# A two-layer mixer trunk whose x, memory and result are laid out feature by feature outside the program

## The reference

```
h      = rms_norm(x) * ln_g
u      = h @ w_in                       # q, k, v, z of four branches, f, and 4 x 1024 gates
mkv    = (rms_norm(mem) * mem_ln_g) @ w_mem_kv
o_b    = attention_b(...)               # stick-breaking, forgetting, dilated, memory
y_b    = (o_b * silu(z_b)) @ w_b
merged = sum over b of sigmoid(gate_b) * y_b
x      = x + merged @ w_out
```

## Time and profile before

| | us |
|---|---|
| median of 3 runs | 1245.41 |
| lowest, highest | 1244.69, 1245.96 |
| the profiled execution | 1244.55 |
| its span, first to last instruction | 1242.8 |
| PE busy in it | 1223.4 (98%) |
| DVE, ACT, POOL busy | 633.5, 681.3, 684.8 |

### The profile page before, as it was taken

One profiled execution on the slowest core, in us unless ns is written; L12 is line 12 of the kernel. 1 busy time (PEld: TensorE's weight loads), 2 busy tenths in 40 slices (PEclk: granted clock), 3 DMA queues, 4 the chain that ended last, 5 costly groups with the idle time before them and its releaser, 6 DMA issues.

```text
span 1242.8 us, 18333 instructions
## 1 busy us (share of the span) xinstructions
PE 1223.4 (98%) x6378; PEld 992.0 (80%) x6378; DVE 633.5 (51%) x1125; ACT 681.3 (55%) x1301; POOL 684.8 (55%) x563
## 2 busy tenths in 40 slices
PE   7999999999999999999999999999999999999998
PEld 6888888777777888887888888887777788888876
DVE  6788533876745222223349874357676442222221
ACT  6775544776554544544458744357755454544531
POOL 3675523574343676776457664237634346776762
PEclk9999999999999999999999999999999999999999
DMA  7654422222222344443365443122222224444342
GB/s 225 171 134 127 102 52 59 60 69 69 65 56 68 98 115 103 106 114 111 102 168 148 126 119 85 44 55 74 60 69 60 60 73 118 102 115 102 103 119 85
DMA packets 209891, 120.83 MB, mean 97 GB/s; under 512 B 9736, under 2 KB 200328, under 8 KB 209800
## 3 DMA queue, kind: packets, MB, share of 16 engines
q1 hardware_dynamic: 209800, 119.66, 37.0%
HBM read 107.04 MB, written 6.29 MB: 91 GB/s over the span
## 4 chain that ended last, share of the span: by engine, by line
PE 92%; DVE 3%; ACT 2%; POOL 1%; issue 1%; DMA 0%; SPq 0%; DVEq 0%; ACTq 0%; POOLq 0%
PE dense L842 76%; PE score L842 6%; PE out L842 4%; PE acc L842 3%; PE acc L1149 1%; PE turn L842 1%; POOL w_lo L1816 1%; POOL dk_lo L1879 1%; PE turn L1000 0%; DMA sig<-in_x 0%; ACT w_hi L1266 0%; PE acc L1000 0%; PE score L953 0%; ACT h_hi L1233 0%; DVE o_norm L1580 0%
## 5 line engine op out<-in xcount | busy, mean ns | idle before, releaser
L1816 POOL TENSOR_TENSOR w_lo<-w_raw,w_hi 128x512 fp32r<-128x512 f32 (+1 forms) x400 | 498.2, 1252 | 519.2 <-ACT w_hi L1266 461.1
L842 PE MATMUL dense<-h_hi,w_hi 128*128 128x512 f32 (+1 forms) x1176 | 473.1, 402 | 2.6 <-DVE h_lo L1457 1.8
L842 PE MATMUL dense<-h_lo,w_hi 128*128 128x512 f32 (+1 forms) x1176 | 457.1, 389 | 0.0
L842 PE MATMUL dense<-h_hi,w_lo 128*128 128x512 f32 (+1 forms) x1160 | 450.9, 389 | 0.0
L842 PEld LDWEIGHTS dense<-h_hi,w_hi 128*128 128x128 f32 x1176 | 221.0, 188 | 59.1 <-issue 11.2
L1266 ACT ACTIVATE w_hi<-w_raw 128x512 fp32r<-128x512 f32 (+1 forms) x401 | 231.6, 585 | 66.2 <-PE dense L842 65.9
L842 PEld LDWEIGHTS dense<-h_hi,w_lo 128*128 128x128 f32 x1160 | 217.7, 188 | 46.7
L842 PEld LDWEIGHTS dense<-h_lo,w_hi 128*128 128x128 f32 x1176 | 221.3, 188 | 39.6 <-issue 0.2
L1552 DVE TENSOR_TENSOR sig<-dense,x_rstd_row 128x512 f32<-128x512 f32 x48 | 33.2, 692 | 215.0 <-issue 122.7
L1326 ACT ACTIVATE sig<-sig 128x512 f32<-128x512 f32 x48 | 30.4, 633 | 127.9 <-DVE sig L1552 127.9
L1554 DVE TENSOR_TENSOR raw<-dense,x_rstd_row 128x512 f32<-128x512 f32 x80 | 54.8, 685 | 29.3 <-issue 18.4
(11 more groups left out here) (297 smaller groups left out, 2030.2 us busy)
## 6 DMA issues: line engine op xcount, KB each, us to landing
w_raw<-in_w_in SPq DMA_DIRECT2D x292, 256.0 KB, 2.9
w_raw<-in_w_out SPq DMA_DIRECT2D x32, 256.0 KB, 2.8
x_scratch<-v_dil SPq DMA_DIRECT2D x16, 256.0 KB, 3.5
w_raw<-in_w_mem_kv SPq DMA_DIRECT2D x16, 256.0 KB, 3.0
v_dil<-x_scratch SPq DMA_DIRECT2D x16, 256.0 KB, 2.8
turned<-normed SPq DMA_DIRECT2D x48, 64.0 KB, 2.5
inv_den<-o_norm SPq DMA_DIRECT2D x48, 64.0 KB, 2.6
silu_z<-in_mem SPq DMA_DIRECT2D x4, 512.0 KB
```

What stands on the lines that cost most here:

```text
L842: return nc.tensor.matmul(o, lhsT, rhs, start=start, stop=stop, skip_group_check=True)
L1816: pool.tensor_tensor(w_lo[:, g % SPLIT_SLOTS, c], w_raw[:, g % RAW_SLOTS, c], f(w_hi[:, g % SPLIT_SLOTS, c]), ALU.subtract).then_inc(w_lo_ ...
```

## The change

1. The host lays out `x`, `mem` and the result with features down; the program loads `x` straight into `xT`, one `kt` at a time, with the first weight item ahead and the second among them. All transposes of `x`, of memory and of the result go. The stores of the result leave from `xT`.
2. Layer 0 makes `h` and the first tile on all 512 tokens. The squares are now made by ACT on `xT` (8 of them) and summed by DVE (7 additions), alternating with `h_hi` and `h_lo`. `x_sum` of layer 0 is the product that layer 1 has, at the table's place, which is inside the first tile.
3. Memory isn't scaled. ACT squares it in four pieces, POOL adds them up (3 additions a layer), PE sums them with two products of 256 columns (`mem_sum`), ACT makes the row of roots, and DVE multiplies it in when it takes `mk` and `mv` from PSUM. `mem_hi` and `mem_lo` are made from SBUF.
4. Layer 0 saves no `x`; it loads it back from the input.
5. The table gets two rooms behind the first `col` and two ahead of the first `rv`; the addition of memory's last gated output goes from POOL to DVE; the last tile of the result is added and stored in two halves.
6. The values' buffers lose their ones (two memsets of POOL).

```
@@ plan_layer
                 yield unit
                 unit = []
+                if s == 0 and e == 0:
+                    yield from [room()] * 2
...
             if s < len(order):
                 yield both("rd", s)
+            if s == 1:
+                yield from [room()] * 2
...
-          [room(), [("x_sum",)]] + [room()] * 6 + [[("mem_square",)]] + [room()] * 2 + [[("mem_scale",)]] + [room()], lag=2)
+          [room(), [("x_sum",)]] + [room()] * 4 + [[("mem_square",)]] + [room()] * 2 + [[("mem_rest",)]] + [room()] * 2 + [[("mem_sum",)]] + [room()], lag=2)
...
-                          ([("mem_t", c)] + ([("mem_low", c - 1)] if c else []), room())] + [[("mem_low", 3)], room()], lag=2)
+                          ([("mem_high", c)] + ([("mem_low", c - 1)] if c else []), room())] + [[("mem_low", 3)], room()], lag=2)
...
-    dense([new("o", None, dt) for dt in range(HALF + 1)])
-    add("out", 0)
-    dense([new("o", None, dt) for dt in range(HALF + 1, KT - 1)])
-    dense([new("o", None, KT - 1)], [room(), [("out", 1)]])
-    add("out", 2)
+    dense([new("o", None, dt) for dt in range(KT)])
@@ sync
-                    if n in saves:
+                    if n in saves and l:
...
+            for kt in range(KT - 1):
+                sp.wait_ge(*x_new.of(kt))
+                sp.dma_start(out[:, kt, :], xT[:, kt, :]).then_inc(out_stored, 16)
+            for i in range(2):
+                c = slice(i * MEM, (i + 1) * MEM)
+                sp.wait_ge(x_last, i + 1)
+                sp.dma_start(out[:, KT - 1, c], xT[:, KT - 1, c]).then_inc(out_stored, 16)
@@ tensor
                         if l:
-                            wait(pe, turn_ring.before("x_sum"))
                             pe.wait_ge(*x_summed.of(KT - 1, ago=1))
-                            mm(T[:, :], ones, turned[:, :], start=True, stop=True).then_inc(x_total.sem, 1)
                         else:
...
+                            pe.wait_ge(first_summed, KT - 1)
+                        mm(T[:, :], ones, turned[:, :], start=True, stop=True).then_inc(x_total.sem, 1)
+                    elif kind == "mem_sum":
+                        wait(pe, turn_ring.before("mem_sum"))
+                        pe.wait_ge(*mem_added.of(3))
+                        for i in range(2):
+                            last = mm(T[:, 0:MEM], ones, sig[:, 0, i * MEM:(i + 1) * MEM], start=i == 0, stop=i == 1)
+                        last.then_inc(mem_total.sem, 1)
@@ scalar
             first_split(0)
             act.wait_ge(params_in, 16 * DEPTH)
             first_high(0)
+            first_high(1)
+            first_square(0)
+            first_high(2)
             first_split(1)
+            for kt in range(3, KT):
+                first_square(kt - 2)
+                first_high(kt)
             first_split(2)
+            first_square(KT - 2)
+            first_square(KT - 1)
@@ vector
             for kt in range(KT):
+                first_low(kt)
+                if kt >= 3:
+                    first_add(kt - 2)
+            first_add(KT - 2)
+            first_add(KT - 1)
...
+                            if t.branch == MM and t.idx == KT - 1:
+                                a = acc[t.idx % 2][:, :]
+                                dve.wait_ge(*y_gated.of(t.n))
+                                dve.wait_ge(*y_added.before(t.n))
+                                dve.tensor_tensor(a, a, gated[gated_ring.slot(t.n)], ALU.add).then_inc(y_added.sem, 1)
@@ gpsimd
+                    elif kind in ("mem_square", "mem_rest"):
+                        for c in (1, 2) if kind == "mem_square" else (3,):
+                            pool.wait_ge(*mem_squared.of(c))
+                            if c >= 2:
+                                pool.wait_ge(*mem_added.of(c - 1))
+                            pool.tensor_tensor(sig[:, 0, :], sig[:, 0, :], mem_square_place(c), ALU.add).then_inc(mem_added.sem, 1)
```

More of the change, by code:

```diff
@@ L781, in _ @@
             stage = flat(probs[:, :, :])
+            sp.dma_start(stage[:, 0:P], c_square[:, IDENT, :]).then_inc(const_in, 16)
             sp.dma_start(stage[:, P:9 * P].rearrange("p (a b) -> p a b", b=P), c_square[:, HEADSUM:, :])\
@@ L903, in qk_there @@
                     once(qk_lo_ready.of(tile_at[kind, branch, idx]))
-                def first_tile():
-                    for u in range(2):
-                        c = slice(u * MEM, (u + 1) * MEM)
-                        for kt in range(KT):
-                            half, i = divmod(kt, HALF)
-                            if u == 0 and i == 0:
-                                pe.wait_ge(w_lo_ready, half + 1)
-                            pe.wait_ge(first_h_lo[u], kt + 1)
-                            part = slice(i * P, (i + 1) * P)
-                            last = three(dense_bank[0][:, c], w_hi[:, half, part], w_lo[:, half, part],
-                                         h_hi[:, kt, c], h_lo[:, kt, c], u == 0 and kt == 0, u == 1 and kt == KT - 1)
-                            if u == 1 and i == HALF - 1:
-                                last.then_inc(w_used, 1)
                 for s in steps:
@@ L921, in _ @@
                     if kind == "x_sum":
+                        once((setup, 2))
+                        wait(pe, turn_ring.before("x_sum"))
                         if l:
-                            wait(pe, turn_ring.before("x_sum"))
                             pe.wait_ge(*x_summed.of(KT - 1, ago=1))
-                            mm(T[:, :], ones, turned[:, :], start=True, stop=True).then_inc(x_total.sem, 1)
                         else:
-                            pe.wait_ge(first_squares, TT)
@@ new lines, in _ @@
+                    elif kind in ("mem_square", "mem_rest"):
+                        act.wait_ge(mem_in, 64 * (l + 1))
+                        for c in range(3) if kind == "mem_square" else (3,):
+                            if c == 3:
+                                act.wait_ge(*mem_added.of(1))
+                            act.activation(mem_square_place(c), memT[:, c, :], ACT.Square).then_inc(mem_squared.sem, 1)
+                    elif kind == "mem_sum":
+                        act.wait_ge(*mem_total.of(0))
+                        act.activation(mem_rstd_row[:, :], T[:, 0:MEM], ACT.Ln, scale=1.0 / D, bias=eps).then_inc(mem_rstd.sem, 1)
+                        act.wait_ge(*mem_rstd.of("ln"))
+                        act.activation(mem_rstd_row[:, :], mem_rstd_row[:, :], ACT.Exp, scale=-0.5).then_inc(mem_rstd.sem, 1)
@@ L1510, in _ @@
                     kind = s[0]
-                    if kind == "out":
-                        if l < DEPTH - 1 or s[1] == 1:
-                            continue
-                        a = s[1] // 2
-                        for i in (0, 2):
-                            dve.wait_ge(out_turned, a * TT + i + 1)
-                            dve.tensor_copy(token_stage(i)[:, a * S:(a + 1) * S], (R[0], O)[i // 2][:, :])\
-                                .then_inc(out_copied[0], 1)
-                    elif kind == "mem_low":
+                    if kind == "mem_low":
                         c = s[1]
@@ L1583, in _ @@
                                 dve.wait_ge(x_back, 16 * KT * (l + 1))
+                            if (l, t.idx) == (DEPTH - 1, KT - 1):
+                                for i in range(2):
+                                    c = slice(i * MEM, (i + 1) * MEM)
+                                    dve.tensor_tensor(xT[:, t.idx, c], bank_[:, c], xT[:, t.idx, c], ALU.add).then_inc(x_last, 1)
+                                continue
                             dve.tensor_tensor(xT[:, t.idx, :], bank_[:, :], xT[:, t.idx, :], ALU.add)\
@@ L1855, in _ @@
                         pool.tensor_tensor(cosine_place(t), normed_place(t), rope[:, 0, :], ALU.mult).then_inc(cos_done.sem, 1)
-                    elif kind == "post1" and s[1].kind == "y" and s[1].branch != DIL and not last_y(s[1]):
+                    elif kind == "post1" and s[1].kind == "y" and s[1].branch != DIL and not last_y(s[1]) \
+                            and (s[1].branch, s[1].idx) != (MM, KT - 1):
                         t = s[1]
@@ L1905 @@
           for k, v in arrays.items()}
-    result = nc.dram_tensor("result", (S, D), F32, kind="ExternalOutput").ap()
+    result = nc.dram_tensor("result", (P, KT, S), F32, kind="ExternalOutput").ap()
     def rows_split(w):
@@ L1917 @@
     r = run_bass_kernel_spmd(nc, [arrays], core_ids=[0])
-    return r.results[0]["result"].reshape(1, S, D)
+    return r.results[0]["result"].reshape(P, KT, S).transpose(2, 1, 0).reshape(1, S, D)
```

236 lines of the change are left out of this document (67 added, 169 removed).

## The result

| | before | after |
|---|---|---|
| median of the runs, us | 1245.1 (4 runs beside those of after) | 1257.1 (4 runs) |
| lowest, highest | 1244.7, 1246.0 | 1256.8, 1257.9 |
| ratio, 95% interval | | 1.0097 (1.0085 to 1.0109) |
| the profiled execution, its span | 1244.55, 1242.8 | 1257.44, 1255.6 |

A forecast was written before the change was run, and what follows sets the result against it. PE, busy 98% of the span, was taken as the bound. Terms -1.4 (memory), -3.1, -2.2, -2.2, -0.6 make -9.5, with the head +1.6 -7.9: 1236.7, stated as 1237.0 us for the median; range 1232.5 to 1241.

The forecast's parts named there:

- Turning the result: Result transposes out 0 and out 1, between dense matmuls on PE: their removal saves 1.76 and 1.33 us, -3.1.
- memory's transposes: Four groups of four transposes on PE in each of two layers, 0.455 us each: their removal gives -3.6 us.
- The sum: All terms added: -9.5, or -7.9 with the head at +1.6; 1236.7 plus 0.9 for the median, stated as 1237.0 us.
- The end: From DVE's last addition to the span's end: half additions and split stores save 2.2 us, between 1.6 and 2.8.
- The last sum: PE's wait for the last sum, 0.6 us a layer, shrinks with memory's last addition on DVE: -0.6, half of -1.2.
- The head: Start of layer 0: PE waits at x_sum until 17.9 us, then runs at half speed, losing 2.5 us; net +1.6.
- two products for +2.2: mem_sum on PE, two plain float32 products of 256 columns a layer: 1.1 us a layer, +2.2, at most 3.5.
- The 20 gaps that become a triple shorter: Table places shortened by the rooms, 0.68 us each: PE shows no wait of size there, so nothing taken.
- The rival that had it in view: Shortened table gaps: 40 lose 0.68 us, 27 us if none had slack, 1264; decides from 16 on; chance 0.05.
- The table: Rooms at the second col and first rv remove PE waits of 0.7 and 0.4 us in each layer: -2.2.
- DVE behind POOL's additions: Rival, 50 to 75 us: three additions a layer cost DVE 0.65 us each, 1240; chance 0.20 shared with no table help.
- The signs named as wrong: PE waiting for raw<-dense between 50 and 110 us, new waits at sb_sum or rv, or squares done before 14 us.

The follow-up runs named there:

- e3: The changed kernel with layer 0's x_sum run on PE after 36 matmuls, in the middle of the second tile, not after 15: 1251.5 us.
- e4: The changed kernel with mem_sum in a score bank, the last two sb_sum together and layer 0's x_sum after 36 matmuls: 1239.45 us.
- e1: The changed kernel with mem_sum's two products put into a score bank of PSUM, not the turn bank: 1254.8 us.
- e2: The changed kernel with the two sb_sum steps of the last stick-breaking block standing together in the table: 1248.2 us.
- e7: The kernel before with only the two rooms behind the first col added: 1252.6 us, ratio 1.0056.
- e8: The kernel before with only the two rooms ahead of the first rv added: 1244.6 us against 1244.8.
- e10: e9 with the three additions of memory's squares in each layer on DVE, not POOL: 1235.3 us.
- e12: e4 with squares' additions on DVE, mem_high and mem_low at places 20 to 45, squares at 93 to 111, mem_low reading ACT's PSUM copy: 1234.6 us.
- e9: e4 with ACT copying memory into a score bank of PSUM, from which DVE's mem_low reads: 1237.8 us.
- e5: e4 with the mem_high and mem_low steps moved into the first group of tiles, the squares ahead of them: 1239.4 us.

## Why the prediction was wrong

- **Turning the result, -3.1; memory's transposes, -3.6.** The rows are gone, and nothing took their place on PE. Right by the trace; no run had them alone.
- **The sum.** 1236.7 and 0.9 are 1237.6, not 1237.0: a slip of 0.6, small beside the 20 us.
- **The end, -2.2.** It gave 3.6: 3.1 us from DVE's last additions, not 4.5. The stores were issued 1.3 us after the additions began (1.45 forecast), the queue waited 1.4 us for the last landing and not 2.3, and the span ends 0.5 behind that, not 0.7.
- **The last sum, -0.6.** PE's wait for the low part of the last sum, 0.6 us in each layer, is no longer in its list, so it is nearer to -1.2. Its row stands beside other edits, so this is not separated.
- **The head, +1.6.** It cost 2.75 us (24.70 against 21.95). The mechanism was that of the forecast, waiting and then half speed, but the wait was 6.05 us and not 4.5. Mis-sized is the chain of DVE: its last addition ended at 19.8 and not at 17.9. DVE waited 2.6 us for `h_hi` of the next three `kt`, not 0.7 (the second `kt` was there at 6.85), and its last three additions took 3.35, not 2.1, since the last square had to wait for a place that an addition frees. Half speed lost 1.7 us (nine matmuls from 20.98 to 24.70 for 2.05), not 2.5. `e3` shows that PE needn't wait there at all: in `e4` PE's first head sum starts at 27.2 us, in the kernel before at 30.2, in after at 32.9.
- **Memory: two products for +2.2, at most 3.5 "if both halves wait for POOL's last addition".** The first of two steps that failed. The products themselves were not the error: in `e4`, layer 0, they cost 0.87 us (53.15 to 54.47, less two pitches) for 1.1. I asked whether its *input* would be late and never asked who holds its *output* bank. 3.8 us a layer of waiting, and half speed behind it, came from a bank whose reader ACT is a tile behind. `e1` shows the bank as the cause of the wait; what the wait cost in time, it shows at 1.8 us only. The kernel before had put the transposes into the score banks.
- **The 20 gaps that become a triple shorter: "so I take nothing".** The second step that failed, and the costliest: 8.5 us by `e2`, and 7.8 without the rest of the change by `e7`. The rival that had it in view got 0.05 and was priced as 40 gaps of 0.68 us, to decide from 16 of them on. It was not a shorter gap that cost, but one pair of steps with two foreign steps slipped in between, and one such place in each layer is enough: its price is the length of the chain that slipped in (3 us, and half speed behind it), not the shift (0.68). "Only the two mended places show a wait" was no argument, since the other places had slack only in the order that they had.
- **The table, -2.2.** The wait at `col` and that at `rv` went as forecast. What the first brought is not shown, since `e7` has the new wait with it; of the 0.8 us for `rv`, `e8` shows 0.2, with an interval that holds both nothing and 0.8.
- **DVE behind POOL's additions, 0.65 each, 1.5 a layer.** Seen as a rival and in the right stretch, but too small and on the wrong operation: I noted that `mem_low` now reads SBUF and put no price on it. Eleven of its sixteen products took 1.0 us more, 5.7 us a layer. In after little of it showed in PE's waits, with the pauses there; in `e4`, without them, PE has some 7 us of new waits (w_lo 3.9 for 1.9, raw 2.8, square 2.2), and `e10` is 5.6, `e12` 6.3 us better than `e4`.
- **The clock.** A wait on PE has a second price that I had applied at the head alone. After a pause of 3 to 4 us PE ran at half speed for up to 6.2 us more (911.80 to 918.02, behind `sb_pv` of layer 1), and seven matmuls at 0.43 us lose 1.4.

The signs named as wrong came true in part: a new wait in the stick-breaking part, though at `sb_pv`, and in `e1` and `e4` PE's waits for `raw<-dense`.

## What to carry to other kernels

When a step is put into a fixed order, ask of both of its ends: who still holds the buffer that it writes, and not only whether its inputs are there. When units in such an order move by one place, list which pairs of steps that belong together now have a foreign step between them, and price each with the foreign step's whole chain. And when an operand moves from PSUM to SBUF, take the new operation's duration from a row with the same places for its operands and with POOL busy beside it, above all if it stands ahead of the step that frees a bank for PE.

## What the runs showed of the hardware

- A DVE product of 256 columns with both tensors in SBUF took 476 ns where POOL stood idle as it started and about 1.5 us (median 1504) where POOL was at work; with one in PSUM it took 472 (469 to 478) in the same stretch of the kernel before, and 474 in `e9`. A copy on ACT into PSUM, 512 columns at a time, bought that back at no cost that could be seen.
- Six additions moved from POOL to DVE made the kernel faster by 2.7 and 2.5 us, and DVE's own busy time fell by 1.9 and 2.1 us. In layer 0 POOL had begun them between 30 and 50 us, where DVE was busy for 75% in `e5` and 72% in `e9` (25 to 50 us); in the 25 us behind, it was busy for 97% in `e5`.
- The pause at `sb_pv` in layer 0 (2.94 us) was followed by some seven matmuls at 1.2 GHz in after, 0.43 us apart, and the same pause (2.93) by none in the profiled execution of `e1`, 0.23 apart. So a pause of this length went either way. The granted clock of each run, which is on record, says the same: `e1` had one run of 1252.9 us at 0.997 and three of 1254.7 to 1255.7 at 0.992 or 0.993, `e7` one of 1249.1 at 0.999 and three of 1252.4 to 1253.4 at 0.994 or 0.995. PE's timeline of `e1`:

```profile
293.95 1.08 PE L834 MATMUL out<-probs,v_tok 128*64 128x512 f32 x4 [2.93 <-ACT probs L1361]
295.29 0.39 PE L834 MATMUL dense<-h_lo,w_hi 128*128 128x512 f32 x1
295.52 0.40 PE L834 MATMUL dense<-h_hi,w_lo 128*128 128x512 f32 x1
```
